# Seven products of halves for gate b and the silu branch in both blocks, with the next chunk's GLU gate as filler

## The reference, cut to what matters

```python
proj = u @ w_in                                  # 9 x 1024 columns
a_b, a_c, a_h, a_z, b_v, b_g, b_z, gate_a, gate_b = split(proj)
s  = a_c * a_h
ya = (a_b * dwconv3(s, history_a) * silu(a_z)) @ w_out_a
v  = b_v * sigmoid(b_g)                          # GLU
c  = dwconv31(v, history_b) + bias
yb = (silu(LayerNorm(c)) * silu(b_z)) @ w_out_b
m  = sigmoid(gate_a) * ya + sigmoid(gate_b) * yb
h  = x + m @ w_o
y  = RMSNorm(h + sigmoid(RMSNorm(h) @ w_pg) * (p @ w_pe))
```

## Time and profile before

| what | value |
|---|---|
| runs of the kernel before | 970.2, 850.99, 852.25 us; median 852.25 us |
| profiled execution: device time | 851.9 us |
| profiled execution: span of the slowest core (core 1) | 850.4 us (others 845.5 to 848.8 us) |
| TensorE busy | 828.0 us, 97% |
| VectorE busy | 545.5 us, 64% |
| ScalarE busy | 348.4 us, 41% |
| granted TensorE clock, mean of core 1 | 0.996 |

### The profile page before, as it was taken

The page is one execution under the profiler, slowest core; times in us unless marked ns, Lnnn a source line. Parts: engine busy times, 40 slices in busy tenths (PEclk is TensorE's granted clock), DMA queues, the critical chain, the costliest instruction groups (busy, mean ns, idle before and its releaser), DMA issues.

```text
span 850.4 us, 17021 instructions; the slowest of 8 cores (845.5 to 850.4 us)
## 1 busy us (share of the span) xinstructions
PE 828.0 (97%) x5678; PEld 482.9 (57%) x5678; DVE 545.5 (64%) x822; ACT 348.4 (41%) x558; POOL 214.0 (25%) x404
## 2 busy tenths in 40 slices
PE   8899999999989999999999999999999999999995
PEld 3677777777767777776444444444444444444442
DVE  3535678666965875556686565666767595556566
ACT  4212323322246665442675123333334554332554
POOL 3541333323301122122443322212221202200112
PEclk9999999999999999999999999999999999999999
DMA  8999999999965987989995898888997638994533
GB/s 240 148 171 197 179 164 175 162 165 143 169 137 82 248 116 177 211 166 229 255 247 143 148 153 135 146 144 143 147 141 117 131 56 137 160 189 154 149 89 116
DMA packets 91134, 135.57 MB, mean 159 GB/s; under 512 B 37528, under 2 KB 45992, under 8 KB 89000
## 3 DMA queue, kind: packets, MB, share of 16 engines
q0 software_dynamic: 33392, 57.72, 44.8%
q1 hardware_dynamic: 57512, 76.50, 40.6%
q10 hardware_dynamic: 144, 0.26, 0.1%
HBM read 169.26 MB, written 19.35 MB: 222 GB/s over the span
## 4 chain that ended last, share of the span: by engine, by line
PE 88%; DMA 5%; DVE 2%; issue 2%; ACT 1%; SPq 1%; POOL 0%; POOLq 0%; DVEq 0%; ACTq 0%
PE ps L635 34%; PE ps L1161 20%; PE ps L1065 16%; PE ps L1353 7%; PE ps L1409 7%; PE ps L782 4%; DMA t_cbuf<-x 2%; PE ps L1401 2%; DMA t_reg<-vsd 1%; DMA t_ring<-w_in 1%; DMA vd<-t_vt 1%; SPq L747 0%; DVE t_uT L612 0%; SPq L754 0%; PE ps L849 0%
## 5 line engine op out<-in xcount | busy, mean ns | idle before, releaser
L635 PE MATMUL ps<-t_uT,t_ring 128*128 128x288 bf16 (+1 forms) x2176 | 326.1, 312 | 3.2 <-DVE t_uT L612 2.4
L635 PEld LDWEIGHTS ps<-t_uT,t_ring 128*128 128x128 bf16 x2176 | 212.0, 98 | 114.5 <-issue 8.1
L410 POOL DMA_DIRECT2D t_ring<-w_in x144 | 78.8, 550 | 263.9 <-PE ps L635 142.8
L1161 PE MATMUL ps<-t_yaT,t_ring 128*128 128x288 bf16 (+1 forms) x384 | 64.9, 317 | 0.0
L1161 PE MATMUL ps<-t_cbuf,t_ring 128*128 128x288 bf16 (+1 forms) x384 | 64.9, 317 | 0.0
L1161 PE MATMUL ps<-t_uT,t_ring 128*128 128x288 bf16 (+1 forms) x384 | 64.2, 317 | 0.0
L1409 PE MATMUL ps<-t_reg,t_mis 128*128 128x512 bf16 x272 | 61.5, 379 | 0.5 <-ACT t_cbuf L1423 0.5
L1076 ACT ACTIVATE ps<-ps 128x288 f32<-128x288 f32 (+1 forms) x56 | 27.5, 490 | 83.7 <-PE ps L1065 83.4
L1353 PE MATMUL ps<-t_cbuf,t_yaT 128*128 128x512 bf16 x272 | 61.4, 379 | 0.4 <-DVE t_yaT L1259 0.4
L446 ACT ACTIVATE t_tmp<-t_cbuf 128x1024 bf16<-128x1024 f32 x37 | 38.8, 1049 | 39.2 <-DVE t_cbuf L1434 37.0
L1161 PEld LDWEIGHTS ps<-t_yaT,t_ring 128*128 128x128 bf16 x384 | 37.2, 98 | 22.3 <-issue 1.3
(11 more groups left out here) (155 smaller groups left out, 1191.0 us busy)
## 6 DMA issues: line engine op xcount, KB each, us to landing
t_ring<-w_in POOLq DMA_DIRECT2D x144, 256.0 KB, 7.5
t_xs<-x SPq DMA_DIRECT2D x30, 512.0 KB, 6.0
y<-t_cbuf SPq DMA_DIRECT2D x16, 512.0 KB, 3.5
t_reg<-vd SPq DMA_DIRECT2D x32, 132.0 KB, 5.6
t_reg<-vd SPq DMA_DIRECT2D x32, 131.9 KB, 6.3
t_reg<-vd SPq DMA_DIRECT2D x32, 131.9 KB, 6.9
t_reg<-vd SPq DMA_DIRECT2D x32, 131.9 KB, 7.7
t_ring<-w_cv POOLq DMA_DIRECT2D x16, 256.0 KB, 9.6
```

Of the source, the lines that this page charges most:

```text
L410: S.add("pool", lambda e, k=k, src=src: e.dma_start(out=ring[k][:, :], in_=src), writes=[f"ring{k}"], dma=f"ring{k}")
L635: S.add("pe", lambda e, k=k, si=si, c0=c0: e.matmul(ps[:, b + si, 0:wb], lhsT=ring[k_][:, 128 * k:128 * k + 128], rhs=src[:, k, c0:c0 + wb ...
L1161: S.add("pe", lambda e, k=k, si=si, c0=c0: e.matmul(ps[:, b + si, 0:wb], lhsT=ring[k_][:, 128 * k:128 * k + 128], rhs=src[:, k, c0:c0 + wb ...
```

## The change

In the first block chunks 2 to 6 now go through `s3_pair` as well (chunks 0, 1 and 7 don't). In both blocks the filler of `g_core` is no longer the convolution of chunk j-1 but the GLU gate projection of chunk j+1 (`gate2`, and `gate_gen(0)`, the first gate_a projection, for the last chunk of the second block). The convolution of chunk j-1 follows in one piece. `s2_late(j+1)` then needs the value projection only. In the first block the 3-tap convolution of chunk j moves into its own core, its first tap (`s3_tap0`) to ScalarE. us0 to us3 are made around chunk 1, where before they were spread over chunks 2 to 4 and the end of the stage; us2 gets another place (`us_far`) and is made again at the end (`us_near`). `sample_hist(j+1)` stands behind the convolution now, with one value projection between it and `s2_out(j+1)`.

```diff
+                held2 = {}
+                def gate2(j):
+                    t_ = wuse("in", j, 5)
+                    for u in range(U):
+                        b = palloc()
+                        yield from halves(t_, uT, u_res, u, b)
+                        t, r = talloc()
+                        S.add("act", lambda e, b=b, t=t: e.activation(out=two(t), in_=pp(b), func=AF.Tanh, scale=0.5),
+                              reads=pres(b), writes=[r])
+                        held2[j, u] = t, r
+                        yield
+                    wfree(t_)
+
+                def s2_late(j):
+                    use_pairs(*((2, 3) if j == NCH - 1 else (0, 1)) if U == 2 else (0, ))
+                    t_ = wuse("in", j, 4)
+                    for u in range(U):
+                        s2_ev(j, u, proj(t_ % NRING, u), None, held2[j, u])
+                    wfree(t_)
+                    s2_out(j)
...
-                def s3_pair(j):
+                def s3_pair(j, filler):
                     flush(pend_taps)
-                    flush(pend_sums)
+                    if U == 1:
+                        flush(pend_sums)
                     g_weights((3, 0), j, j)
...
+                    if sw:
+                        S.add("pool", lambda e: e.tensor_copy(
+                            out=sexts[:, :, 0:16], in_=hista[:, j, :].rearrange("p (s w) -> p s w", s=2)),
+                            reads=["hista"], writes=["sextsh"])
+                    use_pairs(*((2, 0, 1, 3) if U == 2 else (1 if j > 1 else 0, 3)))
...
                     def fill():
-                        if not taps:
-                            taps.append(s3_tap0(j, 0))
-                        next(cv, None)
+                        if nf[0] % 4 == (1 if U == 2 else 0):
+                            taps.append(s3_tap0(j, nf[0] // 4))
+                        nf[0] += 1
+                        next(filler, None)
...
-                    for _ in cv:
-                        pass
+                    use_pairs(*((0, 1) if j == NCH - 2 else (2, 3)) if U == 2 else (3, ))
+                    s2_conv(j - 1)
...
                 s3_chunk(0)
-                if sw:
+                if bi:
+                    s3_pair(1, gate2(2))
+                else:
                     sample_hist(2)
-                s3_pair(1) if bi else s3_chunk(1)
-                for j in range(2, NCH):
-                    if bi:
-                        use_pairs(3 - j % 2, 0)
-                        s2_proj(j)
-                        s3_pair(j)
-                        continue
-                    s2_conv(j - 2)
-                    s2_proj(j)
-                    s3_chunk(j)
+                    us_far()
+                    us_make(0)
+                    s3_chunk(1)
+                    us_make(1)
+                    s2_conv(0)
+                    us_make(2)
+                    us_make(3)
+                    s2_proj(2)
+                    s3_pair(2, gate2(3))
+                    sample_hist(3)
+                for j in range(2 if bi else 3, NCH if bi else NCH - 1):
+                    s2_late(j)
+                    s3_pair(j, gate2(j + 1) if j < NCH - 1 else gate_gen(0))
                     if sw and j + 1 < NCH:
                         sample_hist(j + 1)
-                    if j < 5:
-                        us_make((0, 1, 3)[j - 2])
+                if not bi:
+                    s2_late(7)
+                    use_pairs(0, 1, 2, 3)
+                    s3_chunk(7)
+                    us_near()
```

96 lines of the change are left out of this document (64 added, 32 removed).

## The result

The changed kernel took 861.8 us (median of 6 runs; before, beside it, 852.9): ratio 1.011, 95% interval 1.009 to 1.013. The forecast was 860, so the time is within 2 us of it, and the sign is right: slower than before, though 40 matmuls are gone and seven convolutions are no longer cut into pieces. The profiled execution spans 862.6 us against 850.4. Of each kernel single executions, like the 970.2 us in the table of before, are longer by up to some 18% at a lower granted clock in one die, and the ratios are of the others.

What follows compares the result with a forecast made beforehand. TensorE was taken as the bound, busy 828.0 of 850.4 us. First block +11.6, clock +1.6 and second block -4.6 gave +8.6 on 851.9 us, rounded down to 860; spread 855 to 866, chance 0.5.

Steps and rivals of the forecast that it cites:

- Part 1: First block, chunks 2 to 6: seven products for eight remove 40 matmuls, saving 4.9 us.
- Part 2: Second block: seven convolutions in one piece instead of four, 0.66 us each, saving 4.6 us.
- Part 3: First block, chunks 1 and 2: VectorE's sums of halves make TensorE wait, together 3.5 us.
- Part 4: First block, chunks 3 to 6: late history load holds GpSimd, then ScalarE and TensorE; 2.2 us per chunk, 8.8 us.
- the threshold: Chunks 3 to 6: TensorE waits only for what the history's landing time exceeds 11.9 us.
- L: Landing time of the sample history load in chunks 3 to 6, taken as 14.1 us.
- the row with the burst: Earlier trace: a history with seven loads issued shortly ahead and no read backs beside it landed in 14.4 us.
- rival A: Chunks 3 to 6: the history lands in time; 847.3 us, or 848.9 with the clock lost once; chance 0.22.
- Rival C: First block: longer waits (landing 15.5 us, 867.5) or clock falling at each (866.9), both 874 us; chance 0.13.
- Part 5: First block, five cores of seven products: small waits for ScalarE's copies, 0.2 us each, 1.0 us.
- Part 6: End of first block: TensorE waits 6 us for chunk 7's read backs; conv(7) starts 11.6 us later than before.
- Part 7: Granted clock falls once, at the longest wait, costing 1.6 us of lost work.

Runs made afterwards that it cites:

- e5: e1 plus separate names for the two halves of the shared temporary `tv`; 853.4 us, 0.999 of before.
- e10: e9 with chunk 7's value product, gate multiplications and writes ahead of conv(5), their reads behind it; 847.8 us, 0.994 of before.
- e3: Changed kernel with the first block's order as in the kernel before, second block as changed; 849.6 us, 0.994 of before.
- e1: Changed kernel with the next chunk's history load issued ahead of the seven products, not behind; 855.9 us, 1.000 of before.
- e11: e10 with GpSimd's weight loads from the end of chunk 6's core held until chunk 7's value write is out; 847.4 us, 0.993 of before.
- e9: Changed kernel with the edits of e1, e5 and e6 together; 850.8 us, 0.997 of before.
- e6: e1 with the four sums of halves on VectorE spread from chunk 0 to chunk 2; 853.5 us, 0.999 of before.
- e4: Changed kernel with a half's taps on VectorE behind both multiplications instead of between them; 865.5 us, 1.012 of before.

## Why the prediction was right, and where it wasn't

The sign was right, and it is new waits that outweigh the matmuls saved, but most of them are not where I had put them. That the total came within 2 us is luck: in core 1, against the earlier trace rows, I had conv(5) 4.2 us too late and the way from there to conv(7) 5.7 us too short. Part by part:

- **Part 1** (4.9 us). Right, a little high. Where no wait stands in a chunk (e5, e10) it lasts 24.85 to 24.91 us against 25.76, so 0.85 to 0.91 of the forecast 0.98 are there.
- **Part 2** (4.6). Right: 7 x 0.67 in the trace, 5.0 (3.5 to 6.6) by e3.
- **Part 3** (1.0, 1.75, 0.8). Right place by place: 1.24, 1.72, 0.65.
- **Part 4** (8.8). This step failed. The chain and the threshold held (12.3 against 11.9), but L was mis-sized: median 10.4 us, not 14.1. It cost 0 to 1.9 us per core in all. I had taken the value near the row with the burst, and rival A's row was nearer. The best row was in the trace of before, and I hadn't split it off: the loads of just these chunks, 3 to 6, landed there in 8.0 to 14.2 us over the eight cores, median 10.2, and in the changed kernel the median to the landing itself is 10.2 again. The median of 12.3 in the earlier trace rows has the three slower loads of the kernel's start in it. So standing behind the burst did not lengthen L in these chunks; what the change took away was the head start that hid it: in core 1 for chunk 6, 12.7 us before from issue to use, and 5.6 now until GpSimd has nothing left to do but wait (187.34 to the end of L735). Rival C's longer L isn't seen in these four chunks: with SyncE's read backs beside them the histories were in sooner than the 14.4 us of the earlier trace rows, where there were none. The rule that stood beside it (the Trainium skill, "DMA: Bandwidth & Descriptors", section on queues, rings and completion order) gave the wrong direction as an estimate of L; whether the engines do take such turns is not tested by this.
- **Left out**: the waits for L1094, 3.0 us. I had gone through the pairs and the copies, not through who reads the shared temporary last. e5 shows the cause: a name, not VectorE's load.
- **Part 5** (1.0). No such waits in these cores of seven products.
- **Part 6.** Conv(5) at 211.5 where I had 215.7; conv(7) at 255.2, 43.7 us later, where I had 253.7, 38 later. This step failed the other way. Of the 5.7 us, 1.1 are the history of chunk 7, used 15.2 us after its issue where I had 14.1. 1.2 are what I had taken off for a median landing. 0.2 stand between the sample store and the first read. The largest piece, 3.2 us, is in the read backs themselves: from the first read to conv(7) 22.6 us (232.64 to 255.24), where before it was 19.35 (222.76 to 242.11) and I had taken it over unchanged. Over the cores, first read to last landing is 17.2 us before, 21.4 in the changed kernel and 17.9 in e1 (medians). Until the history has landed GpSimd issues no weight loads either, and in core 1 four follow right behind it (231.7 to 234.5), beside the reads; e11, where six loads beside the reads went with 21.8 us, fits that as the cause, but no run separates it. The copies behind L739 also hold VectorE's taps, hence the 3.6 us at conv(6), which I had named. e1, which moves the five loads and nothing else, gives 9 us, most of it behind conv(5).
- **Part 7** (1.6). Too small. 1.7 us behind conv(6)'s wait and 1.9 in conv(7), which came at half clock; the half of rival C about the clock took place twice, though not at the waits of under 2 us in the cores of seven products.

Summed for core 1: conv(7) +13.1, from conv(7) to the statistics of the block (L851) +2.8 (17.64 to 20.42, mostly clock), second block to its own statistics -5.8 (404.9 to 399.1; 4.7 of it part 2, the rest small waits in the first block's gates that are gone), the rest +0.3: +10.4, the difference of the spans (860.8 and 850.4).

Of the marks that I had set, two came out as forecast (chunks 3 to 6 last 25.6 to 27.5 us in core 1, and the second block has no waits) and one by half: the landing's median is 12.8 us in the slowest core, but under 12 (9.6 to 11.1) in cores 2, 5, 6 and 7. Those medians are over all eight loads, and so too high for the chunks that the argument is about.

**What the first block hangs on.** It is the chain from chunk 7's value write to the last landing of its read backs, for which conv(7) waits. Up to e9 it starts behind conv(5). An earlier conv(5) starts it earlier too, so a gain there should be kept. In e5 and e6 it wasn't, because the chain itself took longer: 24.9 us in e1 (median of the cores), 27.9 in e5, 27.2 in e6, 25.9 in e9. Most of the difference stands between the value write and the first read (6.7, 9.6, 9.5, 8.5). So e5's -3.6 us up to conv(5) came back as +3.2 behind it. In e10 the chain starts ahead of conv(5); it is about as long as in e9 (26.3 us), and that gain was kept. Open is why the value write's landing took longer in e5 and e6 than in e1, with the same loads issued ahead of it; a fuller queue of transfers is my guess, and one execution each doesn't rule out chance.

**The best version** is e10 (or e11): 0.994 of before, 1.7% under the changed kernel. Against e3, which has only the second block's half (0.994), it is not better by more than can be measured. So seven products for eight in the first block are worth about nothing in time at this size: 2.4 us between conv(0) and conv(7) (165.3 to 162.9), less what comes back behind.

## What to carry to other kernels

When a step moves, follow its DMAs in the queue that issues them. Here a load that was asked for behind a core of products and not ahead of it cost as much as the whole change was to bring (9 us), and nothing in the busy shares showed it. To size a landing, take the rows of the same chunks, not the median over the whole kernel. Before counting the worth of a shorter stage, look for the stage's last wait and measure the chain that ends there in each version: it can take back a gain by growing, and loads held back from one of its links can end up beside the next (e11). And where the program derives waits from names, one name for two regions is a wait: give it away before reordering (e4 moved the wait, e5 removed it).

## What the runs showed of the hardware

- The same load of history (core 1, chunks 3 to 7) landed in 3.7 to 6.7 us in e1 and in 9.6 to 15.1 in the changed kernel; a write of 264 KB landed in 2.5 or in 7.9 us (core 0 of e11 and of e9), with fewer or more loads issued shortly before. Here a landing time belonged to a place in the order more than to a transfer.
- A VectorE instruction of 128x576 (L838) took 1.14 us beside GpSimd's doubling in the three places above, and at most 0.76 wherever the two didn't overlap.
- In core 1, after waits of 3.6 and 6.4 us the granted clock fell (0.66, 0.50); after waits of 1.2 to 1.9 us inside the stream of products it stayed at 1.00, though 1.66 us at the kernel's start had been followed by 0.50. Other cores of the changed kernel show that length alone doesn't decide it: 1.97 us at conv(6) in core 3 was followed by a granted clock of 0.50, and 3.36 us at conv(7) in core 2 was not. What made the difference no run here shows. The reading of the Trainium skill ("TensorE: Matmul & The Clock Gate", Part 1) that I had put beside rival C, that each new wait could bring the low clock, held in core 1 for the two longest waits and for none of the short ones.
